# Three products of split operands in place of f32 products for two groups of projections

## The reference, cut to what matters

```python
for l in range(2):
    h = rmsnorm(x, norm_mix_g)
    z_r, z_h, z_s, z_g = split(h @ w_in)                 # one combined input projection
    z_r = token_shift(z_r, h_prev @ w_in[:, :RWKV_COLS], shift_mu)
    ...                                                  # RWKV-7, HGRN2 and gMLP branches, gates
    x = x + merged @ w_out
    h = rmsnorm(x, norm_ffn_g)
    q = (h @ peer_wq).reshape(tokens, 8, 2, 128)         # the query projection
    s = einsum("thpd,hpnd->thpn", q, peer_keys)          # scores, then top-k over them
    ...                                                  # PEER: gated single-neuron experts
    x = x + experts
y = rmsnorm(x, norm_final_g)
```

## Time and profile before

| | |
|---|---|
| median of 3 runs | 3104.83 us (3104.26 to 3105.77) |
| the profiled execution's own time | 3104.68 us |
| its span, first to last instruction | 3102.9 us |
| mean granted TensorE clock | 0.96 |
| PE busy | 2879.6 us (93%) |
| DVE, ACT, POOL busy | 1784.0, 1068.5, 527.9 us |
| share of PE in the chain that ended last | 62% |

### The profile page before, as it was taken

One profiled execution on the slowest core, in us unless ns is written; L12 is line 12 of the kernel. 1 busy time (PEld: TensorE's weight loads), 2 busy tenths in 40 slices (PEclk: granted clock), 3 DMA queues, 4 the chain that ended last, 5 costly groups with the idle time before them and its releaser, 6 DMA issues.

```text
span 3102.9 us, 54395 instructions
## 1 busy us (share of the span) xinstructions
PE 2879.6 (93%) x20890; PEld 2655.3 (86%) x20890; DVE 1784.0 (57%) x2785; ACT 1068.5 (34%) x1744; POOL 527.9 (17%) x220
## 2 busy tenths in 40 slices
PE   7899778899999999999998996798999999999998
PEld 5788557789999999999976885577899999999997
DVE  1754654229856666666627537532497566666665
ACT  1212211025544335555403112100355433455553
POOL 0000020018842220000000001100288322200000
PEclk9999888999999999999999998789999999999999
DMA  5222212334543335555451222113354433455553
GB/s 198 94 71 69 89 40 82 122 104 162 162 143 122 121 119 173 182 177 182 154 198 66 82 69 85 58 68 136 110 162 163 130 121 121 129 178 180 180 179 122
DMA packets 114363, 395.92 MB, mean 128 GB/s; under 512 B 18195, under 2 KB 19731, under 8 KB 112853
## 3 DMA queue, kind: packets, MB, share of 16 engines
q1 hardware_dynamic: 105444, 381.28, 37.4%
q10 hardware_dynamic: 8816, 13.27, 1.4%
HBM read 385.44 MB, written 8.53 MB: 127 GB/s over the span
## 4 chain that ended last, share of the span: by engine, by line
PE 62%; issue 22%; POOL 8%; DVE 6%; ACT 1%; DMA 0%; POOLq 0%; ACTq 0%; SPq 0%; DVEq 0%
PE bank L418 62%; POOL WHL L1732 8%; DVE arena L1220 4%; ACT arena L899 1%; POOL arena L1728 1%; DVE arena L1318 0%; DVE arena L1434 0%; DVE hT L1228 0%; ACT L899 0%; DVE arena L1224 0%; DVE arena L1228 0%; DVE NRM L1238 0%; DVE arena L1283 0%; DVE arena L1450 0%; DMA COM<-com 0%
## 5 line engine op out<-in xcount | busy, mean ns | idle before, releaser
L418 PE MATMUL bank<-HHL,WHL 128*128 128x264 f32 x6144 | 795.5, 288 | 27.6 <-POOL WHL L1732 21.9
L418 PEld LDWEIGHTS bank<-HHL,WHL 128*128 128x128 f32 x6144 | 763.6, 190 | 37.9 <-POOL WHL L1732 29.0
L418 PE MATMUL bank<-AHL,WHL 128*128 128x264 f32 x6144 | 748.7, 284 | 0.0
L418 PEld LDWEIGHTS bank<-AHL,WHL 128*128 128x128 f32 x6144 | 748.5, 188 | 0.0
L899 ACT ACTIVATE WHL<-raw 128x1024 fp32r<-128x1024 f32 x512 | 542.3, 1060 | 336.1 <-PE bank L418 334.4
L1732 POOL TENSOR_TENSOR WHL<-raw,WHL 128x1024 fp32r<-128x1024 f32 x188 | 485.3, 2589 | 1013.2 <-ACT WHL L899 1013.2
L418 PE MATMUL bank<-hT,ring 128*128 128x264 f32 (+1 forms) x2496 | 595.9, 397 | 14.2 <-DVE hT L1228 11.7
L418 PEld LDWEIGHTS bank<-hT,ring 128*128 128x128 f32 x2496 | 476.8, 193 | 107.6 <-DVE hT L1228 12.5
L1220 DVE TENSOR_TENSOR WHL<-raw,WHL 128x1024 fp32r<-128x1024 f32 x324 | 395.0, 1219 | 26.2 <-ACT WHL L899 26.2
L418 PEld LDWEIGHTS bank<-arena 64*64 64x64 f32 (+3 forms) x3200 | 268.6, 162 | 136.6 <-DVE arena L1220 97.8
L418 PE MATMUL bank<-arena 64*64 64x64 f32 (+7 forms) x3200 | 294.1, 252 | 96.4 <-DVE arena L1220 89.1
(11 more groups left out here) (108 smaller groups left out, 1397.4 us busy)
## 6 DMA issues: line engine op xcount, KB each, us to landing
raw<-down SPq DMA_DIRECT2D x256, 512.0 KB, 3.5
raw<-up SPq DMA_DIRECT2D x256, 512.0 KB, 3.5
ring<-wm SPq DMA_DIRECT2D x100, 1024.0 KB, 5.0
arena<-hs ACTq DMA_DIRECT2D x2, 1280.0 KB, 6.1
o_hs<-arena ACTq DMA_DIRECT2D x2, 1280.0 KB, 4.5
arena<-cm SPq DMA_DIRECT2D x2, 1160.0 KB
arena<-rs SPq DMA_DIRECT2D x4, 512.0 KB, 8.3
o_rs<-arena ACTq DMA_DIRECT2D x4, 512.0 KB, 5.1
```

Of the source, the lines that this page charges most:

```text
L418: return pe.matmul(out, lhsT, rhs, start=start, stop=stop)
```

## The change

Mixer tiles 1 to 24 and query tiles 2 to 15 are computed as the expert units are: 24 fp32r matmuls of split operands instead of 16 records of f32. Tiles 0 of the mixer, 0 and 1 of the query, and mixer tiles 25 to 37 stay as they were. ACT copies each weight tile's high part to one of three buffers (`WZ`, `WQ`; `w_hi`), three tiles ahead. The low part is subtracted in place in the ring: by DVE for mixer tiles 1 to 13 and all query tiles (`w_low`), by POOL for mixer tiles 14 to 24 (`w_plow`). `HH` holds the split activations of the mixer and lies over the sample state's place, so SP loads `SR` at pair 17 instead of pair 7, now behind the wait for the ring. The query uses `HHL`, which was there. `hT`'s split, the buffers and the ring's fp32r view get memory of their own or that of buffers not yet in use.

```diff
@@ SP
-                    if p == 7:
+                    if slot in last:
+                        name, n = used(last[slot], l)
+                        sp.wait_ge(S[name], n)
+                    if p == 17:
                         for half in range(2):
                             sp.dma_start(SR[64 * half:64 * half + 64], d["rs"][l][:, half * VH:(half + 1) * VH, :])\
                                 .then_inc(S["sr_in"], 16)
-                    if slot in last:
-                        name, n = used(last[slot], l)
-                        sp.wait_ge(S[name], n)
@@ PE
+            def proj_split(out, slot_tile, high, src, low_sem, low_n):
+                for q in range(2):
+                    for k in range(KD):
+                        mm(out, high[:, k, :], src[q][:, k, :], k + q == 0, False)
+                pe.wait_ge(S[low_sem], low_n)
+                for k in range(KD):
+                    ins = mm(out, ring_r[:, slot_tile, k, :], src[0][:, k, :], False, k == KD - 1)
+                return ins
...
-                        proj(bank[at + c % 2][:, 0:TS], 2 * slot + c % 2, hT, TS).then_inc(S["z_mm"], 1)
+                        if c == 0:
+                            proj(out, tile, hT, TS).then_inc(S["z_mm"], 1)
+                        else:
+                            pe.wait_ge(S["w_low"], l * NLOW + 1)
+                            pe.wait_ge(S["w_hi"], l * NSPLIT + c + 1)
+                            low = ("w_low", l * NLOW + c + 1) if c < RT else ("w_plow", l * 11 + c - RT + 1)
+                            proj_split(out, tile, WZ[c % 3], HH, *low).then_inc(S["z_mm"], 1)
...
-                    proj(bank[n % 2][:, 0:T], 2 * s + n % 2, hT, T).then_inc(S["q_mm"], 1)
+                    if n < 2:
+                        proj(bank[n % 2][:, 0:T], 2 * s + n % 2, hT, T).then_inc(S["q_mm"], 1)
+                    else:
+                        pe.wait_ge(S["hlo_done"], l + 1)
+                        pe.wait_ge(S["w_hi"], l * NSPLIT + 24 + n)
+                        proj_split(bank[n % 2][:, 0:T], 2 * s + n % 2, WQ[n % 3], [HHL[:, 0], HHL[:, 1]],
+                                   "w_low", l * NLOW + 13 + n).then_inc(S["q_mm"], 1)
@@ ACT
+                f(HH[0], hT[:], ACT.Copy).then_inc(S["w_hi"], 1)
+                def w_high(p, half, out):
+                    act.wait_ge(ring_in[ring_pair(p)], ring_count(p, l))
+                    f(out, ring[:, 2 * ring_pair(p) + half], ACT.Copy).then_inc(S["w_hi"], 1)
...
+                for c in range(1, 4):
+                    w_high(c // 2, c % 2, WZ[c % 3])
...
+                        if 1 <= c <= 21:
+                            w_high((c + 3) // 2, (c + 3) % 2, WZ[c % 3])
...
+                for n in range(2, 5):
+                    w_high(41 + n // 2, n % 2, WQ[n % 3])
...
+                    if 2 <= n <= 12:
+                        w_high(41 + (n + 3) // 2, (n + 3) % 2, WQ[n % 3])
@@ DVE, after the sample's shift and ahead of the token shift
+                dve.wait_ge(S["w_hi"], l * NSPLIT + 1)
+                tt(HH[1], hT[:], HH[0].bitcast(F32), ALU.subtract).then_inc(S["w_low"], 1)
+                def w_low(n, p, half, high):
+                    dve.wait_ge(S["w_hi"], l * NSPLIT + n + 1)
+                    at_tile = 2 * ring_pair(p) + half
+                    tt(ring_r[:, at_tile], ring[:, at_tile], high.bitcast(F32), ALU.subtract).then_inc(S["w_low"], 1)
+                for c in range(1, RT):
+                    w_low(c, c // 2, c % 2, WZ[c % 3])
@@ DVE, after HHL
+                for n in range(2, 16):
+                    w_low(24 + n - 1, 41 + n // 2, n % 2, WQ[n % 3])
@@ POOL, first in each layer
+                for c in range(RT, 25):
+                    pool.wait_ge(S["w_hi"], l * NSPLIT + c + 1)
+                    at_tile = 2 * ring_pair(c // 2) + c % 2
+                    pool.tensor_tensor(ring_r[:, at_tile], ring[:, at_tile], WZ[c % 3].bitcast(F32), ALU.subtract)\
+                        .then_inc(S["w_plow"], 1)
```

More of the change, by code:

```diff
@@ L132, in build, with rounded @@
         ARENA = 40336
+        rounded_memory = ExitStack()
+        rounded_at = [0]
+        def rounded(name, off, *dims):
+            if off > rounded_at[0]:
+                rounded_memory.enter_context(nc.sbuf_tensor(name + "_gap", [P, off - rounded_at[0]], F32))
+            rounded_at[0] = off + int(np.prod(dims))
+            return rounded_memory.enter_context(nc.sbuf_tensor(name, [P, *dims], FR))
+        SG_AT, YR_AT, HH_AT = 13456, 15568, 35768
+        WQ = rounded("WQ", 0, 3, KD, P)
+        WZA = rounded("WZA", SG_AT, 2, KD, P)
+        WZB = rounded("WZB", YR_AT, KD, P)
+        HH = rounded("HH", HH_AT, 2, KD, TS)
+        ring_r = rounded("ring_r", ARENA, 2 * RINGP, KD, P)
+        rounded_memory.close()
+        WZ = [WZA[:, 0], WZA[:, 1], WZB[:]]
+        WQ, HH = [WQ[:, n] for n in range(3)], [HH[:, n] for n in range(2)]
         mixer_memory = ExitStack()
@@ L165, in build @@
         o += HT_ * T
+        SGO = o
         SG = at(o, ST, T)
@@ L171, in build @@
         WORK = o
+        assert (SGO, SECOND) == (SG_AT, YR_AT) and HH_AT >= WORK + 12544 + RT * T + 3 * T
+        assert HH_AT + 2 * KD * TS <= ARENA
         AR = at(o, NW, 2, T)
@@ L275, in build @@
             xv_evac zs_ready lora_in lora_mm lora_evac decay_in decay_out kk_sq kk_ss kk_std prep_done bon_done
-            bon_mm mat_mm mat_evac l_mm l_evac p_mm p_evac ml_ready xt_mm xt_add x_mm x_add late_gates x_done tok_mm tok_evac y_mm y_evac u_mm
+            bon_mm mat_mm mat_evac l_mm l_evac p_mm p_evac ml_ready xt_mm xt_add x_mm x_add late_gates w_hi w_low w_plow x_done tok_mm tok_evac y_mm y_evac u_mm
             u_evac o_evac s_mm s_evac sq_mm sq_evac rq_in sr_in sr_done sr_out so_out so_in ot_mm gn_m gn_sq gn_v
@@ L325, in rows4, with ring_pair, ring_count @@
                 .broadcast_to([ap.shape[0], ap.shape[1], n, ap.shape[2]])
+        def ring_pair(p):
+            return p % RINGP if p < 37 else (p - 37) % RINGP
+        def ring_count(p, l):
+            return 16 * (l * USES[ring_pair(p)] + sum(ring_pair(q) == ring_pair(p) for q in range(p + 1)))
+        NSPLIT, NLOW = 1 + 24 + 14, 1 + 13 + 14
         block = ctx.enter_context(nc.Block())
@@ L462, in z_tiles @@
                         pe.wait_ge(S["z_evac"], l * 38 + c + 1)
-                        proj(bank[at + c % 2][:, 0:TS], 2 * slot + c % 2, hT, TS).then_inc(S["z_mm"], 1)
+                        out, tile = bank[at + c % 2][:, 0:TS], 2 * slot + c % 2
+                        if c == 0:
[5 more added lines that the diff above has]
+                            proj_split(out, tile, WZ[c % 3], HH, *low).then_inc(S["z_mm"], 1)
                         if c % 2:
```

## The result

The changed kernel takes 3089.66 us (median of 7 runs, 3085.86 to 3096.09), the kernel before beside it 3105.50 (7 runs, 3104.26 to 3111.84). The ratio is 0.9946, 95% interval 0.9936 to 0.9956: 14 to 20 us faster. The forecast was 3084.3, its range 3070 to 3095, with 0.94 for faster. Time and sign are inside; of the 20.4 us that the sum promised, about 15 are to be seen in the profile (span 3102.9 to 3087.8), and the next sections say where the rest went.

The account below looks back on a forecast made before the run. PE was taken to bound the query stage and mixer tiles 0 to 13, DVE's chain the stretch up to the chunk products. 3104.68 - 18.0 (query) - 2.4 (mixer) = 3084.3 us; range 3070 to 3095.

Parts of the forecast that it names:

- the sum: Whole kernel: 3104.68 us less 18.0 for the query and 2.4 for the mixer, giving 3084.3 us.
- The query term: Query stage, 14 tiles a layer: each 0.64 us shorter, PE waiting for nothing; 9.0 us a layer, 18.0 for two.
- the mixer term: Mixer stage: shorter tiles, mostly offset by POOL's low parts delaying DVE; 1.2 us a layer gained, 2.4 for two.
- the second rival: LoRA products: PE's pauses for low parts 18 and 19 lower its clock, 3 us a layer; 3090, up to 3096; chance 0.13.
- I take 2.92 and keep 3.00: Mixer tile, 24 fp32r matmuls of 272 columns: 2.92 us assumed, 3.00 in proportion to columns kept as the bound.
- The first rival: Mixer: POOL and DVE run side by side at no cost, 11.4 us a layer reach the chunks; 3064; chance 0.13 for under 3078.
- the third: Mixer: all ten low parts 15 to 24 stand on DVE's chain at 2.4 us each; 3111.7, slower; chance 0.03.
- the fourth: Query stage: matmuls wait tile by tile for low parts, so the 18 us go and 3102 is left; chance 0.03.

Follow-up runs that it names:

- POOL's work on other data: Changed kernel without POOL's low parts; POOL does eleven unused subtractions of the activations at their places, PE waiting for none during the tiles: 3091.34 us, ratio 0.9942.
- with tiles 1 to 13: Changed kernel with only mixer tiles 1 to 13 split, tiles 14 to 24 in f32, POOL idle in the mixer, query part kept: 3078.54 us, ratio 0.9897.
- the copies: Kernel before plus one or two useless DVE copies of V a layer ahead of the reciprocal of DVE's chain: 3110.98 us (ratio 1.0004) and 3115.28 us (1.0022).
- the run with two copies: Kernel before plus two useless DVE copies of V a layer ahead of the reciprocal of DVE's chain: 3115.28 us, ratio 1.0022.
- the filling: Kernel with mixer tiles 1 to 18 split and all low parts on DVE, plus 14 useless PE matmuls behind mixer tile 24: 3063.29 us, ratio 0.9856.

## Why the prediction was right, and where it was not

*The query term held.* 18.0 us were taken and 18.1 measured: tiles 2.91 to 2.94 us apart, nothing waited for. It has to be read over the whole fourth stretch: from the second norm to the first top 16 alone it is 10.1 us, because the norm itself comes 1.1 us later behind the start of the stretch (129.66 us against 128.52), where no code was changed.

*The mechanism of the mixer term held, step by step.* The token shift was to be stretched by 7.0 us and was by 6.6; low parts 22 to 24 were to cost DVE's chain 6.5 us and cost 6.3 (2.04 in the scan, 4.06 in the operations at 112.32, 0.22 in the first scale); tile 1 was to stall 0.4 us and stalled 0.23. The runs without POOL's low parts, with POOL's work on other data and with tiles 1 to 13 show that these turns are what most of the gain was lost to. PE waited for low parts 18 and 19, 1.40 and 2.79 us, where the second rival had some 2 and 3. The wait for low part 19 stands beside the turns: tile 19 and with it the LoRA products come some 0.6 us after tanh and its neighbours were ready, which the run with POOL's work on other data gets back (77.2 against 77.8 us from the norm to the LoRA products).

*That its size came out, 0.2 and 1.2 us for the 1.2 taken, is in part luck.* Three terms were wrong. "I take 2.92 and keep 3.00" chose the wrong end: 24 matmuls of 272 columns take 125.0 ns each, in proportion to the columns, and 13 x 0.08 = 1.0 us of the gain is not there. Against it, the sum took 101.45 for tanh, but there ACT only loads its table, and needs no token shift for it; tanh itself began at 102.74. Before and in the changed kernel:

```profile
102.74 0.87 ACT L899 ACTIVATE arena<-arena 64x264 f32<-64x264 f32 x2
...
94.51 0.87 ACT L954 ACTIVATE arena<-arena 64x264 f32<-64x264 f32 x2
```

So there was 1.3 us more to gain, and from PE's first tile (31.07 before, 31.74 now) tanh came 8.9 us earlier, close to the 8.5 of the sum because the two errors cancel. And the high copy of tile 22 with the wait for tile 19 costs 1.0 us between tanh and DVE's first scale (5.33 before, 6.33 now), not 0.5. That leaves 8.9 - 1.0 - 6.3 = 1.6 us. In the first layer 1.3 of them are missing ahead of tile 0: the small product, which the change does not touch, takes 6.51 us instead of 5.17, at a granted clock of 0.57 (the windows above), and 0.2 are left. In the second layer it takes 5.4 us, as before and with the same copy of ACT beside it, but the LoRA products run at the lower level, and 1.2 are left. The four other layers with this code gain 0.4, 0.4, 0.7 and 1.2.

*What failed is a sentence that the prediction did not write:* that unchanged code keeps its length. 5.3 us of the profiled execution, and most of what lies between 3084.3 and 3089.7, were lost in the three stretches behind the chain and the query. The sum started from a profile in which the stretch to the gating norm had its shorter length in both layers. The second rival had the mechanism, PE at the lower clock behind its rests, but put it on the LoRA products at 3 us a layer. It does fall on them, in ten of the twelve layers of the runs with tiles 1 to 19 or more split (in one of them for part of the products only), the changed kernel's second layer among them:

```profile
1624.80:1638.10 13.30, 13.30 (x33) 9.50 (x34) 8.66 (x12) 7.85 (x17) 5.60 (x3) 0.50 0.23 79
97.90:105.60 7.70, 7.70 (x33) 5.86 (x34) 4.72 (x4) 7.26 (x17) 6.08 (x3) 1.00 0.42 136
```

13.3 us at 0.50 against 7.7 at 1.00, but only the first four of 16 products hold up DVE's first scale, by 1.4 us. The larger part of the loss fell on chunks, levels and norms, one to two microseconds at a place. The spread over a kernel's runs (10 us here, 8 before) goes the same way: of the 19 runs of the kernel before beside the copies, the five under 3107 us have a mean granted clock of 0.959 or 0.960, the longest, 3113.86, has 0.957. It is shown that the granted clock makes the difference (one layer against the other in the same execution), that it needs no change in the code (the small product of the run with two copies), and that PE's rest is its condition at the chunk products (the filling). Which combination of lengths a run gets stays open, and so does whether the change makes the longer ones more frequent: the stretch to the gating norm is over 127.7 us in 12 of 20 layers with some part of the change, and in one of six without.

*The first rival* (no cost of the port) is out by the run of the mixer part alone, *the third* (POOL holds everything) by the time, *the fourth* by the query's tiles.

## What to carry to other kernels

An idle engine is not free when its operations take turns with those of the busy one: price each meeting from the trace and compare with doing the same work on the busy engine. When an engine is made faster in one stage, look at which of its tiles end a wait; the eleven behind the token shift cost more than they gave. And give the forecast of a kernel with many short PE rests a margin for unchanged code (here one to two microseconds at a place), or try to fill the rests, as paid at the one place where it was tried. When a sum comes out, check its terms too: here two errors of a microsecond hid each other.

## What the runs showed of the hardware that was not expected

- A low part of POOL that waits behind DVE's long two-input operations is shown at 5.4 to 6.1 us instead of 2.40, and DVE's 4.0 us operation at 6.1: both lose, DVE 2.1 us of POOL's 2.4.
- fp32r matmuls of 272 columns follow one another at 125.0 ns, of 264 at 121.5. The Trainium skill, TensorE: Matmul & The Clock Gate (Wait — 56ns, not 53.3ns?), would give 115.8 ns by estimate for 272 columns; here the measurement decides.
- The same 32 matmuls behind the same wait of 1.53 us take 2.14 or 3.65 us within one execution, and 14 useless matmuls in a wait of 6.1 us made the kernel 8.1 us faster by the profiles' spans.
